# Gates, branch products and their merged sum of a fused two-block kernel, laid out by features instead of tokens

## The reference

```python
h = rmsnorm(x, norm1_g[i])
z = h @ w_in[i] + b_in[i]
_, _, mv, mo, mi, mf, rq, rk, rv, rg, gm, gr = split_cols(z)
...
y_m = (jax.nn.sigmoid(mo) * head_layernorm(hm, m_norm_g[i], M_HEADS))
y_r = (jax.nn.silu(rg) * head_layernorm(hr, r_norm_g[i], R_HEADS))
merged = jax.nn.sigmoid(gm) * (y_m @ w_bm[i]) + jax.nn.sigmoid(gr) * (y_r @ w_br[i])
x = x + merged @ w_out[i]
h2 = rmsnorm(x, norm2_g[i])
x = x + jnp.square(jax.nn.relu(h2 @ w_ff1[i] + b_ff1[i])) @ w_ff2[i] + b_ff2[i]
```

## Time and profile before

| what | us |
|---|---|
| median of three runs | 2323.59 (2323.38 to 2324.47) |
| the profiled execution | 2322.39 |
| its span, first to last instruction | 2320.2 |
| TensorE busy | 2259.6 (97%) |
| weight loads of TensorE, beside its matmuls | 1943.9 (84%) |
| VectorE busy | 1481.8 (64%) |
| ScalarE busy | 1021.1 (44%) |

### The profile page before, as it was taken

How to read it: one execution, slowest core, us unless ns; L and a number is a source line. 1 busy time by engine, 2 the same in 40 slices (tenths; PEclk the granted TensorE clock), 3 DMA queues, 4 the chain that set the end, 5 groups by cost and what they waited for, 6 DMA issues and landing times.

```text
span 2320.2 us, 33051 instructions
## 1 busy us (share of the span) xinstructions
PE 2259.6 (97%) x14188; PEld 1943.9 (84%) x14188; DVE 1481.8 (64%) x1878; ACT 1021.1 (44%) x1238; POOL 27.7 (1%) x52
## 2 busy tenths in 40 slices
PE   6998999999999999999999999999999999999997
PEld 4775677777787878999989877999998987789997
DVE  4677553333336567665778767675678876768576
ACT  4255441112225346434664445443466534445444
POOL 0000000000000000000000000000000000000000
PEclk9999999999999999999999999999999999999999
DMA  8540034444423252455565554555556555455553
GB/s 332 200 163 1 19 145 190 173 160 185 163 94 125 92 143 74 165 199 200 206 234 190 186 187 145 182 184 198 194 179 236 195 184 195 148 181 182 193 190 108
DMA packets 56505, 389.98 MB, mean 168 GB/s; under 512 B 6688, under 2 KB 7080, under 8 KB 11176
## 3 DMA queue, kind: packets, MB, share of 16 engines
q1 hardware_dynamic: 51848, 370.56, 43.8%
q0 software_dynamic: 4512, 17.31, 2.5%
HBM read 386.79 MB, written 1.06 MB: 167 GB/s over the span
## 4 chain that ended last, share of the span: by engine, by line
PE 80%; DVE 11%; ACT 5%; issue 2%; DMA 2%; SPq 0%; POOL 0%; DVEq 0%; ACTq 0%
PE PS L514 24%; PE PS L516 24%; PE PS L515 24%; DVE w_lo L1708 2%; DMA raw<-chunks_in 2%; PE PS L857 2%; PE PS L1032 1%; ACT w_hi L1235 1%; ACT xn L1313 1%; PE PS L1011 1%; PE PS L730 1%; PE PS L690 1%; DVE BIG L2321 1%; PE PS L755 1%; DVE PS L1928 1%
## 5 line engine op out<-in xcount | busy, mean ns | idle before, releaser
L1708 DVE TENSOR_TENSOR w_lo<-raw,w_hi 128x2048 fp32r<-128x2048 f32 x300 | 684.7, 2290 | 482.8 <-ACT w_hi L1235 480.3
L1235 ACT ACTIVATE w_hi<-raw 128x2048 fp32r<-128x2048 f32 x300 | 572.8, 1916 | 744.0 <-PE PS L516 421.9
L514 PE MATMUL PS<-x_hi_lo,w_hi 128*128 128x256 f32 (+1 forms) x2112 | 635.3, 301 | 3.3 <-DVE x_hi_lo L1773 1.6
L515 PE MATMUL PS<-x_hi_lo,w_lo 128*128 128x256 f32 (+1 forms) x2112 | 632.5, 299 | 0.0
L516 PE MATMUL PS<-x_hi_lo,w_hi 128*128 128x256 f32 (+1 forms) x2048 | 607.4, 297 | 0.0
L514 PEld LDWEIGHTS PS<-x_hi_lo,w_hi 128*128 128x128 f32 x2112 | 397.2, 188 | 28.5 <-issue 10.4
L515 PEld LDWEIGHTS PS<-x_hi_lo,w_lo 128*128 128x128 f32 x2112 | 397.4, 188 | 16.4
L516 PEld LDWEIGHTS PS<-x_hi_lo,w_hi 128*128 128x128 f32 x2048 | 384.9, 188 | 14.0
L514 PE MATMUL PS<-w_hi,x_hi_lo 128*128 128x512 f32 (+1 forms) x800 | 317.1, 396 | 8.0 <-DVE w_lo L1708 7.2
L516 PE MATMUL PS<-w_lo,x_hi_lo 128*128 128x512 f32 (+1 forms) x800 | 313.3, 392 | 0.0
L515 PE MATMUL PS<-w_hi,x_hi_lo 128*128 128x512 f32 (+1 forms) x800 | 312.7, 391 | 0.0
(11 more groups left out here) (318 smaller groups left out, 2209.9 us busy)
## 6 DMA issues: line engine op xcount, KB each, us to landing
raw<-chunks_in SPq DMA_DIRECT2D x348, 1024.0 KB, 4.8
bias_ring<-brows_in POOLq DMA_DIRECT2D x32, 256.0 KB, 3.9
G<-nrows_in POOLq DMA_DIRECT2D x2, 1536.0 KB, 10.6
BIG<-rel_in POOLq DMA_DIRECT2D x4, 512.0 KB, 7.3
free_b<-rel_in POOLq DMA_DIRECT2D x4, 512.0 KB, 8.2
tabt<-tabs_in SPq DMA_DIRECT2D x1, 1280.0 KB, 11.8
X<-x_in SPq DMA_DIRECT2D x1, 1024.0 KB, 8.6
X<-ctx_in SPq DMA_DIRECT2D x1, 1024.0 KB, 10.6
```

What stands on the lines that cost most here:

```text
L514: pe.matmul(o, lhs[0], rhs[0], start=start, stop=False, **more)
L515: pe.matmul(o, lhs[1], rhs[0], start=False, stop=False, **more)
L1235: act.activation(w_hi[:, i % HI_RING, :], ring[:, n % RING, :], ACT.Copy).then_inc(*hi_ready.now(n))
L1708: dve.tensor_tensor(w_lo[:, c % RING, :], ring[:, c % RING, :], w_hi[:, i % HI_RING, :].bitcast(F32), ALU.subtract).then_inc(*lo_ready.now(c))
```

## The change

The gates, w_bm and w_br go over to the feature form, so gm, gr and merged have features on the partitions, and merged is no longer transposed. The gates' bias becomes a column, added inside the sigmoid by ScalarE in four passes of 256 columns; its four bias rows of each layer are no longer broadcast. The high and low halves of merged are made from SBUF by one operation each of 128x1024. The table of columns `colt` grows by 32 floats, which moves all tiles behind it, BIG among them, by 128 bytes; and the second block's tiles in BIG start FF_AT, 192 bytes, above BIG's start. ymT, yrT and ff2T then all start 64 bytes above a multiple of 512, counted from the first weight slot.

```diff
-        ("b_mqk", 32), ("b_rqk", 32), ("conv_w", 128), ...
+        ("b_mqk", 32), ("b_rqk", 32), ("b_g", 32), ("conv_w", 128), ...
...
-        n_big = 12288
+        n_big = 12288 + FF_AT
...
-        rg = big(0, 4096).rearrange("p (t c) -> p t c", t=2)
+        rg = big(FF_AT, 4096).rearrange("p (t c) -> p t c", t=2)
...
-        gm, gr = X_[:, 2048:4096].rearrange("p (t d) -> p t d", t=2), xn[:, 2:4, :]
+        gm, gr = (a.rearrange("p (k t) -> p k t", k=KD) for a in (X_[:, 2048:4096], xn_[:, 2048:4096]))
...
-        ymT = pair_of((bigr(4096, 2048), bigr(6144, 2048)), 256, 8)
-        yrT = pair_of((bigr(0, 4096), bigr(8192, 4096)), 256, 16)
-        merged = SCR[:, :].rearrange("p (t c) -> p t c", t=2)
+        ymT = pair_of((bigr(FF_AT + 4096, 2048), bigr(FF_AT + 6144, 2048)), 256, 8)
+        yrT = pair_of((bigr(FF_AT, 4096), bigr(FF_AT + 8192, 4096)), 256, 16)
+        merged = SCR[:, :].rearrange("p (k t) -> p k t", k=KD)
...
-                    project_tok("gm" if h < 2 else "gr", l, 1, KD, lhs, n0=h % 2, biased=True,
-                                between=at_steps({0: lambda: turn_ym(0)}) if h == 3 else None)
+                    st = "gm" if h < 2 else "gr"
+                    project_feat(st, l, 1, hT[2], n0=h % 2, freed=evicted(st, l),
+                                 between=at_steps({0: lambda: turn_ym(0)}) if h == 3 else None)
...
-                def turn_mg(g):
-                    turn(("mg", l), 4, 2, lambda b, t: merged[:, t, b * P:(b + 1) * P],
-                         ready=lambda t: stored.after("w_br", l, g, 0), b0=4 * g)
-
-                project_tok("w_bm", l, 2, KD, tokens(ymT), need=copied(("ym", l)), between=at_steps({2: lambda: turn_yr(0)}))
+                project_feat("w_bm", l, 2, ymT, need=copied(("ym", l)), freed=gated("w_bm"), between=at_steps({2: lambda: turn_yr(0)}))
                 turn_yr(1)
-                project_tok("w_br", l, 2, 16, tokens(yrT), need=copied(("yr", l), 16),
-                            between=at_steps({0: lambda: turn_yr(2), 1: lambda: turn_yr(3), 6: lambda: turn_mg(0)}))
-                project_feat("w_out2", l, 2, hT_b, freed=updated("w_out2", l), need=copied(("mg", l)), crossed=True,
-                             between=at_steps({0: lambda: turn_mg(1)}))
+                project_feat("w_br", l, 2, yrT, k_tiles=16, need=copied(("yr", l), 16), freed=gated("w_br"),
+                             between=at_steps({0: lambda: turn_yr(2), 1: lambda: turn_yr(3)}))
+                project_feat("w_out2", l, 2, hT_b, freed=updated("w_out2", l), need=copied(("mg", l)), crossed=True)
...
-                bias_rows(l, 4, 12)
+                bias_rows(l, 4, 8)
...
+                    for k in range(4 * j, 4 * j + 4):
+                        at = 16 * l + (8 if st == "gr" else 0) + k
+                        ins = act.activation(buf[:, k, :], buf[:, k, :], ACT.Sigmoid, bias=col("b_g")[:, at:at + 1])
...
-                split_to(first_br + 8)
-                copy_turned(("mg", l), 0, 4)
+                split_to(first_br + 6)
+                merged_high(0)
                 split_to(first_br + 10)
-                copy_turned(("mg", l), 4, 4)
+                merged_high(1)
...
-                        biased("gm", l, 1, wide(gm), h)
+                        scale("gm", h, 2 * h, gm[:, 4 * h:4 * h + 4, :])
...
+                lo_to(first_br + 5)
+                merge_r(0)
+                lo_to(first_br + 7)
+                merged_low(0)
+                lo_to(first_br + 9)
+                merge_r(1)
                 lo_to(first_br + 10)
-                copy_turned(("mg", l), 4, 4)
+                merged_low(1)
```

More of the change, by code:

```diff
@@ L434, in copy_plan @@
                 add(("yr", l), 16, 2, parts(yrT), kind="parts")
-                add(("mg", l), 8, 2, parts(hT_b), kind="parts")
             return plan_
@@ L1196, in bias_rows @@
             def bias_rows(l, n0, n):
-                for b in range(16 * l + n0, 16 * l + n0 + n):
+                for b in range(12 * l + n0, 12 * l + n0 + n):
                     if b >= 2:
@@ L1627, in _, with gates @@
                 in_place("rg", l, 3, rg, ACT.Silu, 1)
-                in_place("gm", l, 2, gm, ACT.Sigmoid)
-                in_place("gr", l, 1, gr, ACT.Sigmoid)
+                def gates(st, j, buf):
+                    split_for(st, l, j)
+                    act.wait_ge(*scaled.after(st, l, j))
+                    for k in range(4 * j, 4 * j + 4):
+                        at = 16 * l + (8 if st == "gr" else 0) + k
+                        ins = act.activation(buf[:, k, :], buf[:, k, :], ACT.Sigmoid, bias=col("b_g")[:, at:at + 1])
+                    ins.then_inc(*tok_acted.now(st, l, j, 0))
+                gates("gm", 0, gm)
+                gates("gm", 1, gm)
+                gates("gr", 0, gr)
                 split_for("gr", l, 1)
                 copy_turned(("ym", l), 0, 4)
-                in_place("gr", l, 1, gr, ACT.Sigmoid, 1)
+                gates("gr", 1, gr)
                 copy_turned(("ym", l), 4, 4)
@@ L1650, in _, with merged_high @@
                     split_to(first_br + 1 + g)
-                split_to(first_br + 8)
-                copy_turned(("mg", l), 0, 4)
+                def merged_high(j):
+                    act.wait_ge(*stored.after("w_br", l, j, 0))
+                    act.activation(hT_b[0][:, 4 * j:4 * j + 4, :], merged[:, 4 * j:4 * j + 4, :],
+                                   ACT.Copy).then_inc(*copied_s.now(("mg", l), j))
+                split_to(first_br + 6)
+                merged_high(0)
                 split_to(first_br + 10)
-                copy_turned(("mg", l), 4, 4)
+                merged_high(1)
                 tails(("n2", l), "w_out2", l)
@@ L1966, in pair_view, with four_of @@
                 return PS[:, 2 * pair:2 * pair + 2, :]
+            def four_of(pair):
+                return pair_view(pair).rearrange("p b (s t) -> p (b s) t", s=2)
             def modulation(l, part):
@@ L2281, in merge_m @@
             def merge_m(l, j):
-                dve.wait_ge(*projected.after("w_bm", l, j, 0))
+                dve.wait_ge(*projected.after("w_bm", l, j, 1))
                 if j == 0:
                     dve.wait_ge(*tok_acted.after("gr", l, 1, 0))
-                cols = slice(j * 512, (j + 1) * 512)
-                dve.tensor_tensor(merged[:, :, cols], pair_view(j), gm[:, :, cols],
-                                  ALU.mult).then_inc(*stored.now("w_bm", l, j, 0))
+                ks = slice(4 * j, 4 * j + 4)
+                dve.tensor_tensor(merged[:, ks, :], four_of(j), gm[:, ks, :], ALU.mult).then_inc(*stored.now("w_bm", l, j, 0))
             def wide(buf):
@@ L2446, in _ @@
                             copy_turned(("ym", l), 0, 4)
-                        biased("gr", l, 1, wide(gr), h - 2)
+                        scale("gr", h - 2, 2 * (h - 2), gr[:, 4 * (h - 2):4 * (h - 2) + 4, :])
                     if h < 2:
@@ L2467, in _, with merge_r, merged_low @@
                 copy_turned(("yr", l), 12, 4)
-                for j in range(2):
-                    if j == 0:
-                        lo_to(first_br + 5)
-                    else:
-                        lo_to(first_br + 8)
-                        copy_turned(("mg", l), 0, 4)
-                        lo_to(first_br + 9)
-                    dve.wait_ge(*projected.after("w_br", l, j, 0))
-                    cols = slice(j * 512, (j + 1) * 512)
-                    link(dve.tensor_tensor(gr[:, :, cols], pair_view(j), gr[:, :, cols], ALU.mult))
-                    link(dve.tensor_tensor(merged[:, :, cols], merged[:, :, cols], gr[:, :, cols], ALU.add),
-                         stored, "w_br", l, j, 0)
+                def merge_r(j):
+                    dve.wait_ge(*projected.after("w_br", l, j, 1))
+                    ks = slice(4 * j, 4 * j + 4)
+                    link(dve.tensor_tensor(gr[:, ks, :], four_of(j), gr[:, ks, :], ALU.mult))
+                    link(dve.tensor_tensor(merged[:, ks, :], merged[:, ks, :], gr[:, ks, :], ALU.add), stored, "w_br", l, j, 0)
+                def merged_low(j):
+                    dve.wait_ge(*copied_s.after(("mg", l), j))
+                    hi, lo = (a[:, 4 * j:4 * j + 4, :] for a in hT_b)
+                    dve.tensor_tensor(lo, merged[:, 4 * j:4 * j + 4, :], hi.bitcast(F32),
+                                      ALU.subtract).then_inc(*copied_v.now(("mg", l), 4 * j + 3))
+                lo_to(first_br + 5)
[4 more added lines that the diff above has]
+                merge_r(1)
                 lo_to(first_br + 10)
-                copy_turned(("mg", l), 4, 4)
+                merged_low(1)
                 def update(st, key, add):
@@ L2635, in lay_out @@
                 chunks.append(weight_chunks(w[:, cuts[n]:cuts[n + 1]]))
-            if n != 4:
+            if n not in (4, 7, 8):
                 brows.append(b[cuts[n]:cuts[n + 1]])
```

15 lines of the change are left out of this document (9 added, 6 removed).

## The result

| what | before | changed |
|---|---|---|
| median, us | 2322.99 | 2337.55 |
| lowest and highest of six each | 2318.72, 2324.47 | 2330.83, 2340.85 |
| ratio, 95% interval | | 1.0073 [1.0057, 1.0088] |
| the profiled execution, its span | 2322.39, 2320.2 | 2338.01, 2336.2 |

The forecast was 2316.2 us and the range ended at 2335.0; the kernel got slower by 14.6 us. Rival (c), 2334.0 us, was the nearest.

The account below looks back on a forecast made before the run. TensorE, 97% busy, was taken as the bound. Turns -3.5, gates -1.1, branches -0.2 and inherited rate -2.6 summed to -7.4 us, on the median 2316.2 us, with an 8-in-10 range of 2314.0 to 2335.0.

Parts of the forecast that it names:

- Rival (c): Matmuls with moving operand in BIG start every 0.1179 us or more, by address: +10.4 us, 2334.0 us; chance 0.23.
- Part 5: Addresses in BIG: tiles starting at 64 instead of 448 above a multiple of 512 were taken to cost nothing.
- Part 4: w_out2 and ff1's first two chunks inherit w_br's fast rate: 1.3 us a layer, 2.6 us in all, saved.
- Part 1: Merged's two transpose groups per layer go, saving 3.5 us; ScalarE and VectorE work in their place costs nothing.
- Part 2: Gates: eight pairs of chunks go 256 wide at 0.1133 us a matmul, saving 1.1 us.
- Part 3: Branch projections w_bm and w_br go 256 wide at 0.1133 us a matmul, saving 0.1 us a layer.
- (a): Branches fast, but hT_b slow by its place, so w_out2 inherits no fast rate: -4.8 us, 2318.8 us; chance 0.19.
- (b): Branches w_bm and w_br draw the slow rate: +0.6 us, 2324.2 us; chance 0.19.
- (d): VectorE or ScalarE, not TensorE, sets the stage; time within 3 us of before; chance 0.03.

Follow-up runs that it names:

- r3: The changed kernel run once more, unedited; 2332.62 us in its one execution.
- e1: The kernel before with only 32 unused floats behind colt, moving BIG and all tiles behind colt by 128 bytes; 2335.45 us, ratio 1.0055.
- e5: The changed kernel with the gate biases in their own tile behind BIG, so tiles of before keep their addresses and BIG's start at 448; 2330.3 us, ratio 1.0039.
- e9: The changed kernel with gate biases in their own tile behind BIG, plus one useless 256-wide matmul ahead of w_out2; 2328.71 us, ratio 1.0039.
- e4: The changed kernel with offset FF_AT set to 0, so BIG's tiles start 384 bytes above a multiple of 512; 2338.55 us, ratio 1.0074.
- r1: The kernel before run once more, unedited; 2325.22 us in its one execution.
- r2: The kernel before run another time, unedited; 2319.97 us in its one execution.
- e12: The changed kernel, gate biases behind BIG, useless matmuls behind ff1's sum of squares and in the first block's second ffn_in; 2313.7 us, ratio 0.9979 to before.
- e11: The changed kernel with gate biases in their own tile behind BIG, plus one useless 256-wide matmul between ff1's and ff2's first halves; 2321.93 us, ratio 1.0001.

## Why the prediction was wrong

**Part 5 failed, and decided the sign.** "I take nothing" was the step. It leaned on three 512-wide products whose stationary operands started at 0, 256 and 448 and that hardly differed, and carried that over to moving operands 256 wide. The rows had the opposite at hand: three rates of one form at one clock. At 64 all 69 chunks out of BIG are slow in the changed kernel and in r3, and 45 of 45 in e1; rival (c) named mechanism, place and price, 3312 matmuls at 0.0046 us or 15.2 us, and deserved more than 0.23. e1's +12.8 us show the price on the old chunks; the 5.2 that the 24 new ones pay are about what the form wins (4.8 at the fast rate).

**Part 4 was right in its term and stopped too early.** Where w_br is fast, w_out2 inherits the rate: from w_out2 to sum 1 e5 takes 32.65 instead of 34.81 us, the turn's 0.87 and 1.3 as forecast. The step that failed is the silent one behind it: that ff1 behind the sum of squares would stay fast, as before. It draws anew there too, and in this form it draws slow: in both layers of all nine traces without a break there, against fast in both layers of the five traces of before with BIG at 448. With BIG's tiles at 448 that takes 31 chunks a layer along, 13 us in all, and it made e5, with each address right, 0.39% slower than before. Why the form turns this draw is open. In the changed kernel first-layer w_out2 is slow (0.1174), behind a slow w_br, but second-layer w_out2 is fast behind an equally slow one: out of BIG at 64 the slow rate is the tile's, and what comes next isn't bound to it.

**Part 1 was right.** w_br's last product and w_out2's first follow each other without a turn, and the low half of merged ends long before the third chunk of w_out2 reads it. The changed kernel's TensorE there, and its VectorE with the low half (L2494):

```profile
1484.26 0.28 PE L515 MATMUL PS<-BIGR,w_hi 128*128 128x256 f32 x1
1484.37 0.28 PE L513 MATMUL PS<-x_hi_lo,w_hi 128*128 128x256 f32 x1
...
1485.83 1.23 DVE L2489 TENSOR_TENSOR SCR<-SCR,xn 128x1024 f32<-128x1024 f32 x1
1487.09 2.29 DVE L1722 TENSOR_TENSOR w_lo<-raw,w_hi 128x2048 fp32r<-128x2048 f32 x1
1489.30 1.22 DVE L2494 TENSOR_TENSOR x_hi_lo<-SCR,x_hi_lo 128x1024 fp32r<-128x1024 f32 x1
```

It ends at 1490.5; the third chunk comes two chunks of 5.6 us behind 1484.37, at 1495.7.

**Part 2 had the wrong rate.** The gates draw after each head's scores, and most draw slow. Changed kernel, TensorE, starts of the first gate pair, of the scores, of the second pair, and of what follows it:

```profile
1351.31 0.36 PE L513 MATMUL PS<-x_hi_lo,w_hi 128*128 128x256 f32 x1
...
1362.70 1.47 PE L1010 MATMUL PS<-BIG 128*128 128x256 f32 x8
1363.92 0.37 PE L513 MATMUL PS<-x_hi_lo,w_hi 128*128 128x256 f32 x1
...
1374.91 0.59 PE L1031 MATMUL PS<-BIG,SCR 128*128 128x512 f32 x1
```

11.39 us for the first pair, 10.99 for the second (10.97 was forecast), 11.09 before. Six of eight chunks in this layer are slow; from the first gate to w_bm it is 0.3 us longer instead of 0.55 shorter. The bound given, 2.7 us more than now, held.

**Part 3** came out within 0.3 us of the forecast where the rate is fast: e5 takes 69.14 us from w_bm to w_out2, before 69.90, of which the turn is 0.87, so that the branches lost 0.1 instead of winning 0.1. In the changed kernel it is 71.61, so the slow rate costs 2.5 us a layer, 4.9 in two; rival (c) had 5.3.

**Sum.** Form alone at right addresses: 2.6 us a layer up to sum 1, of the forecast 3.7. Then come 6.6 a layer lost behind it (e5), or, in the changed kernel's profile, 25.7 us of slow chunks in all, less 4.8 for turns, gates and branches at the fast rate (as forecast) and less the 4.3 at the start: 16.6, where the spans differ by 16.0. Two of these terms are luck of the two executions, 4.8 us for the first block's 22 slow chunks and the 4.3; they nearly cancel, and so do little to the result. Rivals (a) and (b) fell as descriptions: hT_b isn't slow by its place (w_out2 is fast in e5), and the branches don't always draw slow at 448 (24 of 24 chunks fast in e5), though they can: all 12 of e9's first layer are slow. (d) fell with the one wait of 0.6 us.

The Trainium skill ("SBUF — State Buffer", section "SBUF: two separate sides") says that TensorE never waits on another engine. The prediction read from it that every address would cost nothing; that conclusion doesn't agree with e1, where a move by 128 bytes costs 0.55%, with no instruction changed.

## What to carry to other kernels

Count a change of tile sizes as an address change of everything placed behind it, and keep a stream's moving tile where it has been measured (here 448 above a multiple of 512) by putting new tiles last. Where one engine is 97% busy, read its spacing per stream, and try a short break of another kind ahead of a long slow stream: 0.44 us bought 5 to 7 us at a time here, and what follows the break has to be read again, since its rate isn't certain. When one stream's rate changes, look at the next streams as well, since untouched code behind the change lost more than the change won.

## What the runs showed of the hardware

- One form, several spacings at full granted clock: 0.1133, 0.1177, 0.1184 to 0.1188 and 0.1198 to 0.1203 us for 256 columns. With the moving tile at 64 the rate was slow in 183 of 183 chunks (changed, r3, e1); at 384 worse than slow in 69 of 69 (e4); at 448 both rates occur, and the stream keeps the one it enters with. 512 bytes more changed nothing that the ratios show (1.0007, 1.0002).
- With BIG's tiles at 448 the rate of an unbroken stream held over up to 33 chunks, across tiles, and changed only at a break, in all 15 such traces. At 64 and 384 it also changes without a break where the stream enters or leaves BIG: in the changed kernel w_out2 of the second layer is fast right behind a slow w_br. Whether it comes out fast can differ between executions of one program (r1, r2), so that 7 us hang on one draw; with a break there the twelve runs of e12 spread over 8.0 us, the 23 of before beside it over 14.1.
- Open: what makes a draw. Start times across sum 1 read the same to 0.01 us in fast and slow cases, and idle matmuls of one kind were followed by both rates (r1, r2). "Slow w_out2, then fast ff1" and the reverse held in all eleven traces with BIG at 448 and no break behind sum 1 (the nine above, e9 and e11); but which comes from which wasn't tried with a w_out2 made slow, and at address 64 it doesn't hold (slow, slow in the changed kernel's first layer and in r3's second).
